# Two linear recurrences back to back: the first one's norm and gate move into the second's preparation

## The reference, cut to what matters

```python
def chunk_step(state, inp):                      # over 8 chunks, per head
    qc, kc, vc, lfc = inp
    b = jnp.cumsum(lfc, axis=2)
    o_inter = jnp.einsum('bhtd,bhde->bhte', qc * jnp.exp(b), state)
    ...
    o = o_inter + jnp.einsum('bhts,bhse->bhte', att, vc)
    state = (jnp.exp(b_last[:, :, 0, :])[..., None] * state
             + jnp.einsum('bhsd,bhse->bhde', kc * jnp.exp(b_last - b), vc))
    return state, o
...
o = o * lax.rsqrt(jnp.mean(o * o, axis=-1, keepdims=True) + EPS)      # per head
o = o.reshape(bsz, seqlen, HG_W) * norm_g.astype(f32) * jax.nn.silu(g)
```

## Time and profile before

| | |
|---|---|
| median of 3 runs | 3610.48 us (3605.55 to 3614.31) |
| profiled execution, its own time | 3610.87 us |
| its span in the trace | 3609.1 us |
| mean granted TensorE clock | 0.963 of full speed |
| last stage of `hgrn`, first to last instruction | 596.47 to 624.15 us in layer 0, 1941.64 to 1969.15 us in layer 1 |
| preparation stage of `rwkv` | 625.17 to 658.39 us, and 1970.21 to 2003.34 us |

### The profile page before, as it was taken

How to read it: one execution, slowest core, us unless ns; L and a number is a source line. 1 busy time by engine, 2 the same in 40 slices (tenths; PEclk the granted TensorE clock), 3 DMA queues, 4 the chain that set the end, 5 groups by cost and what they waited for, 6 DMA issues and landing times. The chain is left out here.

```text
span 3609.1 us, 49576 instructions
## 1 busy us (share of the span) xinstructions
PE 3374.9 (94%) x21374; PEld 2772.9 (77%) x21374; DVE 1922.9 (53%) x2727; ACT 1194.7 (33%) x1704; POOL 5.5 (0%) x6
## 2 busy tenths in 40 slices
PE   7999996789999999999995779999999988999998
PEld 5888885678788888888884668788887857878886
DVE  4434646745454445444647655453446866447475
ACT  3223432124332233222433124332233264344243
POOL 0000000000000000000000000000000000000000
PEclk9999997779999999999997889999999999999999
DMA  3323221014123232323220014122223202313232
GB/s 124 106 88 108 88 88 59 2 35 136 59 94 105 90 103 90 104 93 102 93 88 4 2 48 134 64 94 100 94 99 117 94 1 77 128 65 103 89 104 72
DMA packets 78202, 301.73 MB, mean 84 GB/s; under 512 B 8947, under 2 KB 9587, under 8 KB 77345
## 3 DMA queue, kind: packets, MB, share of 16 engines
q1 hardware_dynamic: 77984, 298.56, 24.8%
HBM read 296.40 MB, written 6.06 MB: 84 GB/s over the span
## 5 line engine op out<-in xcount | busy, mean ns | idle before, releaser
L315 DVE TENSOR_TENSOR w_lo<-ring,w_hi 128x1024 fp32r<-128x1024 f32 (+1 forms) x508 | 652.7, 1286 | 534.9 <-ACT w_hi L308 534.6
L329 PE MATMUL ps<-xa_hi,w_hi 128*128 128x512 f32 x1728 | 683.7, 396 | 30.7 <-DVE w_lo L315 29.2
L330 PE MATMUL ps<-xa_lo,w_hi 128*128 128x512 f32 x1728 | 676.5, 391 | 0.0
L331 PE MATMUL ps<-xa_hi,w_lo 128*128 128x512 f32 x1728 | 676.5, 391 | 0.0
L308 ACT ACTIVATE w_hi<-ring 128x1024 fp32r<-128x1024 f32 (+1 forms) x508 | 554.6, 1099 | 296.6 <-DMA ring<-in_ffn_in_dram 73.6
L329 PE MATMUL ps<-xb_hi,w_hi 128*128 128x512 f32 x1248 | 489.4, 392 | 0.0
L331 PE MATMUL ps<-xb_hi,w_lo 128*128 128x512 f32 x1248 | 485.8, 389 | 0.0
L330 PE MATMUL ps<-xb_lo,w_hi 128*128 128x512 f32 x1248 | 485.6, 389 | 0.0
L329 PEld LDWEIGHTS ps<-xa_hi,w_hi 128*128 128x128 f32 x1728 | 326.6, 189 | 110.8 <-DVE w_lo L315 30.1
L330 PEld LDWEIGHTS ps<-xa_lo,w_hi 128*128 128x128 f32 x1728 | 327.0, 189 | 68.6 <-issue 1.9
L331 PEld LDWEIGHTS ps<-xa_hi,w_lo 128*128 128x128 f32 x1728 | 326.7, 189 | 68.3
(11 more groups left out here) (353 smaller groups left out, 3509.9 us busy)
## 6 DMA issues: line engine op xcount, KB each, us to landing
ring<-in_ffn_in_dram SPq DMA_DIRECT2D x176, 512.0 KB, 3.4
ring<-in_ffn_out_dram SPq DMA_DIRECT2D x64, 704.0 KB, 4.0
ring<-in_mix_in_dram SPq DMA_DIRECT2D x58, 512.0 KB, 3.4
ring<-in_up_dram SPq DMA_DIRECT2D x44, 512.0 KB, 3.5
ring<-in_w_in_dram SPq DMA_DIRECT2D x22, 512.0 KB, 3.5
ring<-in_down_dram SPq DMA_DIRECT2D x16, 704.0 KB, 4.1
ring<-in_mix_out_dram SPq DMA_DIRECT2D x16, 512.0 KB, 3.5
ring<-in_xk_dram SPq DMA_DIRECT2D x16, 512.0 KB, 3.5
```

Source lines behind the costliest of these rows:

```text
L315: dve.tensor_tensor(core.w_lo[j][:, 0:width], core.ring[j][:, 0:width], core.w_hi[j][:, 0:width].bitcast(F32), ALU.subtract).then_inc(self ...
L329: pe.matmul(out, hi, x_hi, start=(k == 0), stop=False)
L330: pe.matmul(out, hi, x_lo, start=False, stop=False)
L331: last = pe.matmul(out, lo, x_hi, start=False, stop=(k == k_tiles - 1))
```

## The change: what it does

In the last stage of `hgrn` the state is carried by `tensor_tensor_scan`: a row of `state` holds, for each of 64 value channels, its eight chunks next to each other, `falls` is the decay of each chunk copied out to the same shape (zero at chunk 0, which restarts the scan), and one scan for each tile m does state = falls * state + update over 512 columns. `take_updates` therefore writes the updates with the chunk as the innermost index (one element every 32 bytes), and `state_outputs` reads its weights (the state of one chunk, 64 columns) with the same step of 32 bytes. `state_outputs` writes the two heads of a tile into the two halves of one bank, where before each had its own bank, and DVE adds a whole tile at once. PE starts on tile m as soon as scan m is done. The stage ends behind these additions.

The norm and the gate of the first recurrence (squares, sums, root, inverse, spread, two products by tile) move into the preparation stage of `rwkv`, set in between its own instructions.

```diff
@@ hgrn, last stage
-    kv = u[3].rearrange("p (c f) -> p c f", c=NCH)
-    state = core.spare[:, 0:9 * 192].rearrange("p (c f) -> p c f", c=9)
+    kv = u[3].rearrange("p (f c) -> p f c", c=NCH)
+    state, falls, nothing = (core.spare[:, n * U3:(n + 1) * U3] for n in range(3))
+    nothing = nothing[:, 0:C]
+    state_at = lambda m, h, c: (state.rearrange("p (m e c) -> p m e c", m=3, c=NCH)[half(h), m, :, c - 1] if c else
+                                nothing[half(h), :])
 ...
 tensor:
-            pe.wait_ge(carried, 1)
             pe.wait_ge(taken, 4)
             for m in range(3):
-                if m:
-                    pe.wait_ge(copied, m)
-                state_outputs(pe, ps, crossed, state, ..., 2, [m])
-            ... (sums_by_token x3, spread_to_heads x3)
+                pe.wait_ge(carried, m + 1)
+                if m == 2:
+                    pe.wait_ge(copied, 1)
+                state_outputs(pe, ps, crossed, state_at, ..., 2, [m])
 vector:
-            (8 x: state[c + 1] = state[c] * dec[c], linked; state[c + 1] += kv[c], linked)
+            link(dve.memset(nothing, 0.0))
+            link(dve.memset(dv[:, :, 0:1], 0.0))
+            for m in range(3):
+                link(dve.tensor_copy(row(falls, m).rearrange("p (e c) -> p e c", c=NCH),
+                                     dv[:, m, :].unsqueeze(1).to_broadcast([P, C, NCH])))
             dve.wait_ge(taken, 4)
+            for m in range(3):
+                dve.tensor_tensor_scan(row(state, m), row(falls, m), row(u[3], m), 0.0, ALU.mult, ALU.add).then_inc(carried, 1)
             for m in range(3):
                 dve.wait_ge(crossed, m + 1)
                 dve.wait_ge(copied, m + 1)
-                for h in range(2):
-                    dve.tensor_tensor(o[half(h), m, :], o[half(h), m, :], ps[half(h), (2 * m + h + 2) % 8, :], ALU.add)
+                dve.tensor_tensor(o[:, m, :], o[:, m, :], ps[:, 2 + m, :], ALU.add).then_inc(summed_v, 1)
-            ... (reciprocal, 3 x L1782, 3 x L1786)
@@ take_updates
-    dst = kv.rearrange("p (b q r) f -> p b q r f", b=2, r=2)
+    dst = kv.rearrange("p f (b q r) -> p b q r f", b=2, r=2)
@@ state_outputs
-                last = pe.matmul(ps[half(h), (base + 2 * m + h) % 8, c * C:(c + 1) * C], state[half(h), c, m * C:(m + 1) * C],
+                last = pe.matmul(ps[half(h), base + m, c * C:(c + 1) * C], state(m, h, c), q(m, h, c), start=True, stop=True)
@@ rwkv, preparation: vector
             dve.tensor_tensor(norm, kk, kk, ALU.mult).then_inc(squared, 1)
+            dve.wait_ge(o_rooted, 1)
+            dve.reciprocal(o_roots, o_roots).then_inc(o_inverted, 1)
             dve.wait_ge(opened, 3)
 ...
             dve.reciprocal(roots, roots).then_inc(inverted, 1)
+            (3 x: wait o_spread; y = o * hgrn_norm * ps[:, 3 + m, :])
+            (3 x: wait o_scaled; y = y * o_gate)
             dve.wait_ge(spread, 1)
             link(dve.tensor_tensor(three(kk), three(kk), ps[:, 0:3, :], ALU.mult))
 ...
+            dve.wait_ge(o_gated, 3)
             link(dve.tensor_tensor(k_hat, k, e_out, ALU.mult))
@@ rwkv, preparation: tensor
             (L1938 x3)
+            for m in range(3):
+                pe.wait_ge(o_squared, m + 1)
+                sums_by_token(pe, core, 7, m, o_sq[:, m, :]).then_inc(o_summed, 1)
             (L1941 x3, sums of the keys' squares)
+            pe.wait_ge(o_inverted, 1)
+            pe.wait_ge(opened, 6)
+            for m in range(3):
+                spread_to_heads(pe, core, 3 + m, m, o_roots).then_inc(o_spread, 1)
             pe.wait_ge(inverted, 1)
-            pe.wait_ge(opened, 6)
             (spread of the keys' roots)
             pe.wait_ge(rated, 1)
+            pe.wait_ge(o_scaled, 3)
             (bonus sums)
@@ rwkv, preparation: scalar
+            for m in range(3):
+                act.activation(o_sq[:, m, :], o[:, m, :], ACT.Square).then_inc(o_squared, 1)
             (3 sigmoids)
+            act.wait_ge(o_summed, 3)
+            act.activation(o_roots, ps[:, 7, 0:24], ACT.Sqrt, bias=core.eps(), scale=1.0 / C).then_inc(o_rooted, 1)
             (3 copies of the output gate, root of the keys' sums)
+            (exp of e_prev, exp of -cum_w)
+            act.wait_ge(o_scaled, 3)
             act.activation(e_in, cum_w, ACT.Exp).then_inc(grown, 1)
-            (exp of -cum_w, exp of e_prev)
```

More of the change, by code:

```diff
@@ L1707, in hgrn @@
     o = three(u[2])
-    kv = u[3].rearrange("p (c f) -> p c f", c=NCH)
-    state = core.spare[:, 0:9 * 192].rearrange("p (c f) -> p c f", c=9)
[L1710 to L1714, removed]
+    kv = u[3].rearrange("p (f c) -> p f c", c=NCH)
[3 more added lines that the diff above has]
+                                nothing[half(h), :])
+    with stage(nc, "inside", "added", "taken", "copied", "step", "carried", "crossed", "summed_v") as (
+            block, inside, added, taken, copied, step, carried, crossed, summed_v):
         if layer == 0:
@@ L1730, in _ @@
                     (v_n[half(c % 2), c // 2, (2 * m + h) * C:(2 * m + h + 1) * C], att_of(att, m, h, c))], 4, [m])
-            pe.wait_ge(carried, 1)
             pe.wait_ge(taken, 4)
             for m in range(3):
-                if m:
-                    pe.wait_ge(copied, m)
[L1736 to L1744, removed]
+                pe.wait_ge(carried, m + 1)
+                if m == 2:
+                    pe.wait_ge(copied, 1)
+                state_outputs(pe, ps, crossed, state_at, lambda m, h, c: three(qe)[half(h), m, c * C:(c + 1) * C], 2, [m])
         @block.scalar
@@ L1752, in _ @@
                 copy_by_parity(act, ps, m, o, copied, 4)
[L1753 to L1757, removed]
         @block.vector
@@ L1773, in _ @@
                 dve.wait_ge(copied, m + 1)
-                for h in range(2):
[L1775 to L1782, removed]
-                                         ALU.mult, ALU.mult).then_inc(scaled, 1)
-            for m in range(3):
-                dve.wait_ge(scaled, m + 1)
-                dve.tensor_tensor(core.y[:, 2 + m, :], core.y[:, 2 + m, :], g[:, m, :], ALU.mult).then_inc(gated, 1)
-            dve.wait_ge(gated, 3)
+                dve.tensor_tensor(o[:, m, :], o[:, m, :], ps[:, 2 + m, :], ALU.add).then_inc(summed_v, 1)
+            dve.wait_ge(summed_v, 3)
 def sums_by_token(pe, core, bank, m, squares):
@@ L1890, in rwkv @@
     roots = core.small[:, 64:88]
+    o, o_sq, o_roots, o_gate = three(s[2]), three(s[3]), core.small[:, 88:112], big[:, HG:HG + 3, :]
     with stage(nc, "step", "squared", "summed", "rooted", "inverted", "spread", "rated", "bonus_sum", "shifted",
-               "grown", "low_rank", "opened", "cum") as (
-            block, step, squared, summed, rooted, inverted, spread, rated, bonus_sum, shifted, grown, low_rank, opened, cum):
+               "grown", "low_rank", "opened", "cum", "o_squared", "o_summed", "o_rooted", "o_inverted", "o_spread", "o_scaled",
+               "o_gated") as (
+            block, step, squared, summed, rooted, inverted, spread, rated, bonus_sum, shifted, grown, low_rank, opened, cum,
+            o_squared, o_summed, o_rooted, o_inverted, o_spread, o_scaled, o_gated):
         norm, prod, e_in, e_out, e_prev = s[0], s[1], s[2], s[3], s[8]
```

22 lines of the change are left out of this document (11 added, 11 removed).

## The result

| | before | after |
|---|---|---|
| median of 4 runs each | 3608.02 us (3605.2 to 3614.31) | 3583.09 us (3582.41 to 3585.43) |
| profiled execution, its own time | 3610.87 us | 3583.65 us |
| its span | 3609.1 us | 3581.9 us |
| granted TensorE clock | 0.963 | 0.970 |

The ratio is 0.9931, with a 95% interval of 0.9915 to 0.9946: 25 us faster, where 21 were forecast.

What follows compares the result with a forecast made beforehand. The `hgrn` stage was taken as bound by latency, the preparation by DVE's work and one wait. -16.5 + 5.9 = -10.6 us a layer, -21 in two, from 3610.5 to 3589 us; own range 3583 to 3596, wider range 3576 to 3602.

Steps and rivals of the forecast that it cites:

- The preparation, +5.9: Preparation stage of `rwkv`: with the moved steps, the product by `kk` starts 5.9 us later in each layer.
- DVE's stall: Preparation: DVE waits 2.7 us for the root of o's sums before its inverse, everything of DVE queued behind it.
- rival of the early clock: Preparation: PE's clock is high from the moved sums on, so -0.3 us instead of +5.9; 3577 us, chance 0.13.
- The `hgrn` stage, -16.5: Last `hgrn` stage: scans and removal of all behind the additions end it 16.5 us earlier a layer, range -15.6 to -17.5.
- (a): ACT's update copies out of PSUM with a 32-byte step: between nothing and +1.6 us, taken as 0.
- (b): State outputs: PE's weight loads with a 32-byte step stay hidden, as a load may take twice its time; taken as 0.
- mixture of 4.3 us: State outputs: 96 instructions take 4.3 us at mixed clocks, between 5.2 at the low and 2.7 at the high clock.
- (c): State outputs: two heads write one bank's halves at the same time, taken as 0; above, +4.3 us.
- rival (3598): State outputs: the heads take turns at the shared bank, +4.3 us a layer; 3598 us, chance 0.12.
- state outputs longer than 6 us: Sign in the profile after, `hgrn` stage: state outputs above 6 us would show the prediction wrong.
- The moved steps eat the gain: Both stages: ACT's strided writes +1.6, heads by turns +4.3, keys' spread +2.3 leave -2.4 us a layer; 3606, chance 0.06.
- serial weight loads: State outputs: 96 stepped weight loads one by one take 21.4 us, net +6.5 a layer; 3624 us, chance 0.05.

Runs made afterwards that it cites:

- second pair: The kernel before and the changed kernel, both unchanged, profiled once more: spans 3605.4 and 3586.6 us.
- e4: Changed kernel, with DVE waiting for the root of the first recurrence's sums only behind the bonus products; `kk` at 25.8 us, ratio 0.9947 against the kernel before.
- e8: Changed kernel, with pair-matrix products and ACT's logarithm and exponential replacing o's sums, spread and root; 3583.05 us, ratio 0.9929 against the kernel before.
- e7: Changed kernel with e4's edit, the K = 128 products ahead of the moved sums and ACT's gate copies ahead of o's root; ratio 0.9938 against the kernel before.
- e3: Changed kernel, but ACT writes the updates as contiguous runs of 64 (values mixed up); four copies 1.64 us, ratio 0.9942 against the kernel before.
- e1: Changed kernel, but state outputs read 64 neighbouring columns as weights (values mixed up); 3.29 us in layer 1, ratio 0.9942 against the kernel before.
- e2: Changed kernel, but each head writes its own bank and additions go by half tiles; ratio 0.9957 against the kernel before.
- e10: Changed kernel, unchanged, profiled again; median 3588.44 us, ratio 0.9948 against the kernel before.
- e6: Kernel before with only the scans, stepped layouts and shared banks, nothing moved; ratio 0.9983 against the kernel before.
- e5: Changed kernel with the old carry, layouts and banks, so only norm and gate are moved; ratio 0.9950 against the kernel before.
- e11: Changed kernel, layer 0's 3.9 MB transfer issued one stage later; theory A: it delays PE's instruction fetch, so the pause goes; 3586.49 us, ratio 0.9935.
- e12: Changed kernel with e8's edit and layer 0's 3.9 MB transfer issued one stage later; 3583.65 us, ratio 0.9933 against the kernel before.

## Why the prediction was right, and where it was off

*The total.* 3583 us lies in the range 3576 to 3602, 6 us below the forecast. Both stages together gave 7.8 and 9.0 us in the first pair (16.8), 7.4 and 10.6 in the second (18.0), where 10.6 a layer had been forecast (21). In the second pair the spans differ by 18.8, and the two stages are all of it but 0.8. In the first pair the spans differ by 27.2: 16.8 from the stages and 13.7 from the untouched stretches, while the rest of the program was about 3 us longer. The forecast counted nothing outside the two stages. Its 21 us came within 4 of the 25 measured because the stages gave 3 to 4 us less than forecast, while outside them several us came off that the forecast put at nothing. That the two nearly cancel is luck; the terms of the stages are the better test.

*The preparation, +5.9.* Measured: +6.0 / +6.1 in the first pair; `kk` at 25.7 against 25.6. Of its steps: moved sums at the low clock 5.28 us (5.4), DVE's stall 2.53 (2.7), keys' sums 2.79 (2.8), both spreads 7.13 (7.0). L1941's products took 5.47 in place of 4.6, at the low clock to their end. In the second pair PE's products found a higher clock, and the stage was 39.1 and 37.4, 1.2 and 2.9 us shorter from the clock alone, on the way to the rival of the early clock; the moved sums took 5.28 us, at the low clock, there as well. What the prediction left open is which engine the stage waits for. e4 settles it: DVE's stall is not on the path, PE's list is. That fits e8, which takes work from PE, gives some to ACT and shortens the stage, and e7, which only reorders and doesn't.

*The `hgrn` stage, -16.5 (range -15.6 to -17.5).* Measured -13.8 and -15.1, outside the range of this term; 1.2 of the 1.3 us between the layers is the updates (k^T v) at the high clock in layer 1 (1.63 us against 2.84 before), so the change's own part is about -13.8 in both. Layer 1 of the second pair says the same: the updates took 1.63 us in both kernels there, and the stage fell from 27.4 to 13.6. The scans (1.2 us each), the early start of the state outputs (1.5 us behind the last update copy) and the one addition came as forecast. Two of the "three prices that no row shows" were not zero.
- (a) The stepped update copies cost 1.33 us, near the upper bound of 1.6 rather than at "nothing". The "runs of 64" that were taken as the nearest row are not near: e3 shows the whole difference. The Trainium skill's page "Advanced Engine Details and Errata", section "SBUF Cachelines", says that a new cache line on each access is penalised; the copies agree with it.
- (b) The stepped weight loads. The argument was that "a load may take twice its time before it shows". It used the low clock, where an instruction needs 54 ns. They took 58 to 62 ns at either clock: at the low one 0.5 us longer in all (5.9 against 5.4), at the high one twice the 28 ns of the earlier trace rows. In layer 1, where the clock was high, that is 5.60 us against e1's 3.29. The section of the Trainium skill named in (a) fits this as well. The forecast's mixture of 4.3 us was 1.3 to 1.7 short in each layer. It was also taken for both layers from layer 0 alone, while layer 1 of the same trace, with a stage as long, shows 5.38:

```profile
1952.64 5.38 PE L1858 MATMUL ps<-scr,spare 64*64 64x64 f32 x96 [6.49 <-DVEq L1770]
```

- (c) The shared bank: zero was right. e2, with banks apart, ran no faster at the same clock (5.90 us against 5.88). The rule of the Trainium skill's page "TensorEngine Tiling (Array Packing)", section "Restrictions and Gotchas", costs no time in this kernel, where the two heads have different partitions of the bank. That rival (3598) is refuted.

The prediction named state outputs longer than 6 us as a sign that it is wrong. The first pair missed that by 0.03 us; layer 0 of e10 took 8.45 us, 6.24 without its pause.

*The other rivals.* The early clock in the preparation (0.13) came in part, in both layers of the second pair, though not for the moved sums, where the rival had it begin. "The moved steps eat the gain" needed three prices at once, of which one was real. The serial weight loads (0.05, from 155 ns an instruction) were far off at 58 to 62.

## What to carry to other kernels

Moving a latency-bound tail into a stage that has a pause pays by the whole tail, less what it adds to the engine list that the other stage waits for; find that engine by moving a stall, not by its size. A layout that suits one engine (scans want the chunk innermost) is paid by those that read or write it with a step: price it at the high clock, where the slack is smallest. When the clock differs between two executions, compare a stretch that the change doesn't touch before booking the difference, and do it over many executions: one pair can't tell scatter from a small shift.

## What the hardware showed that was not expected

**A weight load with a step of 32 bytes has a rate of its own.** 22 to 23 instructions in a microsecond at clock 0.50 and at 1.00 (58 to 62 ns each); next to each other 24 to 25 at 0.50 and, in e1, 34 at 1.00 with the scans as the bound.

**The clock of a stretch differs between executions of one kernel.** The same 2704 PE instructions behind the preparation took from 123.5 us (0.91) to 135.1 (0.80). With the stages this moves the time by several us, as much as most edits here.

**PE pauses where its next instructions land late.** From the changed kernel run again, layer 0:

```profile
602.81 3.48 PE L1836 MATMUL ps<-scr,spare 64*64 64x64 f32 x54 [1.37 <-DVE spare L1760]
...
608.49 2.77 PE L1836 MATMUL ps<-scr,spare 64*64 64x64 f32 x42 [2.21 <-issue]
```

2.21 us in which PE waited for nothing that the timeline shows, after the 54th of 96 instructions. e1, e2, e3, e6 and e7 have it in layer 0 as well (0.8 to 2.3 us), at the 53rd or 54th instruction; the first execution of the changed kernel, e4, e5, e8 and both executions of the kernel before don't, and with the transfer moved (e11, e12) it was absent both times.

The DMA records of the same traces show what such a pause waits for. A queue named "q8 instruction" carries packets of 16384 bytes, 169 or 170 in an execution. In the 14 profiled executions PE has 99 pauses of more than 0.2 us that end in "issue", and each of the 99 ends 1.2 to 1.6 us behind the end of such a packet. In e10's layer 0 the packet ran from 606.07 to 607.03, and PE went on at 608.49. The DMA view of e10 from 599.0 to 606.0 us (no such packet, only the 3.9 MB transfer), of e10 from 606.0 to 607.1, and of e11 from 599.5 to 600.6:

```profile
q1 hardware_dynamic: 78, 2.40, 105.0%
```

```profile
q8 instruction: 1, 0.02, 5.5%
```

```profile
q8 instruction: 1, 0.02, 5.4%
```

The transfer makes this packet late. In the twelve executions with the transfer in its old place, the packet in question started 5.9 to 9.8 us into the `hgrn` stage of layer 0. Without the transfer (layer 0 of e11 and e12, layer 1 of all) it started 1.3 to 4.7 us into it. The packet itself was hardly slower beside the transfer (1.0 to 1.7 us, once 2.5, against 0.9 to 1.4 in layer 1); it began later. So e11's theory A holds by the packets, while its two executions without a pause would prove little, as 6 of 12 with the transfer had none either. The transfer isn't needed for a pause, though: PE also stopped in the middle of the inner outputs (L1800) in layer 1, for 1.88 us in the changed kernel and 1.6 us in e1, e7 and e10, each time after updates at the high clock and with a packet that had started only 1.0 to 1.1 us into the stage. There it cost nothing, since PE waits for the scans afterwards. Each stretch behind the preparation has two to four such pauses too, in the kernel before as well.
